# Expert weights loaded by halves of the contraction, and one DVE step moved, in a two-layer mixer and mixture-of-experts kernel

## What is computed

```python
def moe(x, router_w, router_bias, w_gate, w_up, w_down, sw_gate, sw_up, sw_down):
    ...                       # 8 of 64 experts for each token, by sigmoid scores in groups
    def expert_block(args):
        b_tok, b_w, e = args
        xb = xt[b_tok]
        h = jax.nn.silu(xb @ w_gate[e]) * (xb @ w_up[e])        # 1024 -> 256
        return (h @ w_down[e]) * b_w[:, None].astype(xt.dtype)  # 256 -> 1024
    ...
    shared = (jax.nn.silu(xt @ sw_gate) * (xt @ sw_up)) @ sw_down
    return (routed + shared).reshape(bsz, s, d)
```

## Time and profile before

| | |
|---|---|
| median of three runs (lowest to highest) | 1270.3 us (1269.92 to 1272.2) |
| the profiled execution: own time, span | 1272.9 us, 1271.2 us |
| PE busy | 1167.8 us, 92% |
| DVE, ACT busy | 486.9 us, 193.4 us |
| DMA | 463.78 MB, 365 GB/s over the span |
| PE clock granted | 0.996 of full on average |

### The profile page before, as it was taken

The page is one execution under the profiler, slowest core; times in us unless marked ns, Lnnn a source line. Parts: engine busy times, 40 slices in busy tenths (PEclk is TensorE's granted clock), DMA queues, the critical chain, the costliest instruction groups (busy, mean ns, idle before and its releaser), DMA issues.

```text
span 1271.2 us, 17795 instructions
## 1 busy us (share of the span) xinstructions
PE 1167.8 (92%) x7237; PEld 569.4 (45%) x7237; DVE 486.9 (38%) x1053; ACT 193.4 (15%) x330; POOL 46.7 (4%) x76
## 2 busy tenths in 40 slices
PE   9999999988889888888899999999888998888886
PEld 7774743433333333332387657333333333333332
DVE  5894633333323222322237255332223233322224
ACT  3231211111111111110122312111111111111102
POOL 6200100000000000000010001000000000000000
PEclk9999999999999999999999999999999999999999
DMA  9775969999999999999953277999999999999993
GB/s 345 200 297 191 421 264 421 421 420 421 421 420 423 422 421 421 423 419 421 401 177 135 103 291 312 369 420 421 420 422 421 421 422 421 422 422 421 421 421 137
DMA packets 76125, 463.78 MB, mean 365 GB/s; under 512 B 8544, under 2 KB 9888, under 8 KB 25376
## 3 DMA queue, kind: packets, MB, share of 16 engines
q1 hardware_dynamic: 75920, 462.37, 89.5%
q10 hardware_dynamic: 144, 0.52, 0.1%
HBM read 456.51 MB, written 6.36 MB: 364 GB/s over the span
## 4 chain that ended last, share of the span: by engine, by line
DMA 47%; PE 46%; SPq 3%; DVE 2%; issue 1%; ACT 1%; DVEq 0%
DMA expert_weights<-in_exp_w_up 43%; PE bank L1115 21%; PE bank L646 4%; PE bank L1150 3%; PE bank L632 3%; PE bank L720 2%; PE bank L736 2%; SPq L303 2%; DMA weight_ring<-in_sh_w_down 2%; PE bank L993 1%; DMA expert_weights<-s_rows 1%; PE bank L747 1%; PE bank L1081 1%; PE bank L1070 1%; PE bank L1042 1%
## 5 line engine op out<-in xcount | busy, mean ns | idle before, releaser
L1115 PE MATMUL bank<-expert_weights,weight_ring 128*64 128x512 f32 x1536 | 342.8, 594 | 34.3 <-DMA expert_weights<-in_exp_w_up 34.3
L1150 PE MATMUL bank<-expert_weights,hiddenT 128*32 128x512 f32 x2048 | 233.0, 595 | 15.7 <-ACT weight_ring L1362 8.5
L1115 PEld LDWEIGHTS bank<-expert_weights,weight_ring 128*64 128x64 f32 x1536 | 123.9, 137 | 246.2 <-issue 245.9
L1968 DVE TENSOR_TENSOR hidden<-silu_gate,bank 128x256 f32<-128x256 f32 x64 | 27.0, 421 | 439.2 <-ACT silu_gate L1371 439.2
L1115 PE MATMUL bank<-expert_weights,hT 128*64 128x512 f32 x512 | 120.3, 612 | 40.2 <-DMA expert_weights<-in_exp_w_up 40.2
L1150 PEld LDWEIGHTS bank<-expert_weights,hiddenT 128*32 128x32 f32 x2048 | 60.7, 109 | 143.0 <-issue 117.7
L1371 ACT ACTIVATE silu_gate<-bank 128x256 f32<-128x256 f32 x64 | 24.6, 385 | 486.0 <-PE bank L1115 486.0
L1115 PEld LDWEIGHTS bank<-expert_weights,hT 128*64 128x64 f32 x512 | 40.2, 139 | 120.6 <-issue 120.6
L1978 DVE TENSOR_SCALAR y_top<-bank,slot_gate 128x512 fp32r<-128x512 f32 x64 | 48.1, 751 | 97.5 <-PE bank L1150 97.5
L1375 ACT ACTIVATE y_top<-bank,slot_gate 128x512 fp32r<-128x512 f32 x64 | 44.0, 688 | 254.6 <-PE bank L1150 254.6
L1985 DVE SCALAR_TENSOR_TENSOR y_low<-bank,slot_gate,y_top 128x512 fp32r<-128x512 f32 x64 | 48.1, 751 | 57.6 <-ACT y_top L1375 57.6
(11 more groups left out here) (375 smaller groups left out, 982.6 us busy)
## 6 DMA issues: line engine op xcount, KB each, us to landing
expert_weights<-in_exp_w_gate SPq DMA_DIRECT2D x128, 1024.0 KB, 15.0
expert_weights<-in_exp_w_up SPq DMA_DIRECT2D x128, 1024.0 KB, 17.1
expert_weights<-in_exp_w_down SPq DMA_DIRECT2D x128, 1024.0 KB, 19.0
weight_ring<-in_w_in_even SPq DMA_DIRECT2D x5, 2048.0 KB, 10.1
weight_ring<-in_w_out SPq DMA_DIRECT2D x4, 2048.0 KB, 7.9
weight_ring<-in_w_in_odd SPq DMA_DIRECT2D x4, 2048.0 KB, 10.4
s_c<-expert_weights SPq DMA_DIRECT2D x1, 3072.0 KB, 9.8
expert_weights<-s_c SPq DMA_DIRECT2D x1, 3072.0 KB, 10.4
```

Source lines behind the costliest of these rows:

```text
L1115: last_mm = nc.tensor.matmul(bank[6][a * 2 * CAP:(a + 1) * 2 * CAP, :].rearrange("p (w f) -> p w f", w=2), octet_tokens(l, v, c)[:, 2 * q ...
L1150: last_mm = nc.tensor.matmul(bank[b][by_tile:by_tile + CAP, :], hm[:, j, own:own + CAP], ew_d(2 * u + a)[:, j, half * 512:(half + 1) * 512 ...
L1968: nc.vector.tensor_tensor(hslot[:, :], sg[:, :], bank[6][:, DE:2 * DE], ALU.mult)\
```

## The change

Gate and up weights are loaded in halves: `expert_half` issues 512 KB for gate and 512 KB for up, chunks 0 to 3 (part 0) or 4 to 7 (part 1), 4 KB for each partition. Part 0 of both experts of a pair comes first and counts on `gu_in[u]`, part 1 on `gu_rest[u]`; `gu_in`, `gu_rest` and `d_in` are now one semaphore for a pair. TensorE waits for `gu_in` ahead of chunk 0 and for `gu_rest` ahead of chunk 4. The refills are written out: `first_refill` issues part 0 once the first four chunks of the first product are done (`gu_half`), part 1 at `gu_full`; `last_refill` also loads the down weights of the last pair in two column halves (`down_half`, rows of 2 KB), and the last down product waits for its second half at `d_rest`. In `dve_mix0` the second half of `dve_s5_inputs` moves behind the decay scores. Extra passes over the experts (`npass` over 1) are not run with these inputs.

```diff
-        def expert_load(sp, m, l, e, s):
+        def expert_half(sp, l, e, s, part, landed):
+
+            lo, hi = part * EW // 2, (part + 1) * EW // 2
             src_g = A["exp_w_gate"][l, e].rearrange("(p c) f -> p (c f)", c=KC)
             src_u = A["exp_w_up"][l, e].rearrange("(p c) f -> p (c f)", c=KC)
-            sp.dma_start(ew[:, s, 0:EW], src_g).then_inc(m["gu_in"][s], 16)
-            sp.dma_start(ew[:, s, EW:2 * EW], src_u).then_inc(m["gu_in"][s], 16)
+            sp.dma_start(ew[:, s, lo:hi], src_g[:, lo:hi]).then_inc(landed, 16)
+            sp.dma_start(ew[:, s, EW + lo:EW + hi], src_u[:, lo:hi]).then_inc(landed, 16)
+
+        def down_half(sp, l, e, s, part, landed):
+
+            src = A["exp_w_down"][l, e].rearrange("(p j) n -> p j n", j=JE)
+            sp.dma_start(ew_d(s)[:, :, part * 512:(part + 1) * 512], src[:, :, part * 512:(part + 1) * 512])\
+              .then_inc(landed, 16)
...
         def first_load(sp, m, l, s):
-            expert_load(sp, m, l, s, s)
-            sp.dma_start(ew[:, s, 2 * EW:3 * EW], down_src(l, s)).then_inc(m["d_in"][s], 16)
+            expert_half(sp, l, s, s, 0, m["gu_in"][s // 2])
+            expert_half(sp, l, s, s, 1, m["gu_rest"][s // 2])
+            sp.dma_start(ew[:, s, 2 * EW:3 * EW], down_src(l, s)).then_inc(m["d_in"][s // 2], 16)
...
+            def refill(base, it, u):
+
+                sp.wait_ge(m["gu_full"], (base - 1) * 2 + u + 1)
+                for part, landed in ((0, m["gu_in"]), (1, m["gu_rest"])):
                     for s in (2 * u, 2 * u + 1):
-                        expert_load(sp, m, l, it * NSLOT + s, s)
-                    sp.wait_ge(m["y_hi_full"], (base - 1) * 2 + u + 1)
-                    for s in (2 * u, 2 * u + 1):
-                        sp.dma_start(ew[:, s, 2 * EW:3 * EW], down_src(l, it * NSLOT + s)).then_inc(m["d_in"][s], 16)
...
+                        expert_half(sp, l, it * NSLOT + s, s, part, landed[u])
+                sp.wait_ge(m["y_hi_full"], (base - 1) * 2 + u + 1)
+                for s in (2 * u, 2 * u + 1):
+                    sp.dma_start(ew[:, s, 2 * EW:3 * EW], down_src(l, it * NSLOT + s)).then_inc(m["d_in"][u], 16)
+
+            def first_refill(ps):
+
+                sp.wait_ge(m["gu_half"], ps + 1)
+                for s in range(2):
+                    expert_half(sp, l, NSLOT + s, s, 0, m["gu_in"][0])
+                sp.wait_ge(m["gu_full"], ps * PAIRS + 1)
+                for s in range(2):
+                    expert_half(sp, l, NSLOT + s, s, 1, m["gu_rest"][0])
...
+            def last_refill(ps):
+
+                sp.wait_ge(m["gu_full"], ps * PAIRS + PAIRS - 2)
+                for part, landed in ((0, m["gu_in"]), (1, m["gu_rest"])):
+                    for s in (2, 3):
+                        expert_half(sp, l, NE - NSLOT + s, s, part, landed[1])
+                sp.wait_ge(m["y_hi_full"], ps * PAIRS + PAIRS - 2)
+                for s in (2, 3):
+                    down_half(sp, l, NE - NSLOT + s, s, 0, m["d_in"][1])
+                for s in (2, 3):
+                    down_half(sp, l, NE - NSLOT + s, s, 1, m["d_rest"])
...
-                        for a in range(2):
-                            pe.wait_ge(m["gu_in"][2 * u + a], 32 * g + 32)
+                        pe.wait_ge(m["gu_in"][u], 64 * g + 64)
                         for c in range(KC):
                             if opening:
                                 pe.wait_ge(m["xg_hi" if c % 2 else "xg_lo"], n + c // 2 + 1)
+                            if c == KC // 2:
+                                pe.wait_ge(m["gu_rest"][u], 64 * g + 64)
...
+                            if opening and c == KC // 2 - 1:
+                                last_mm.then_inc(m["gu_half"], 1)
...
+                            if ending and q == 3 and half:
+                                pe.wait_ge(m["d_rest"], 32 * ps + 32)
...
-            dve_s5_inputs(dve, chain)
+            dve_s5_inputs(dve, chain, 0)
...
+            dve_s5_inputs(dve, chain, 1)
             dve.wait_ge(*B.read("r1"))
```

More of the change, by code:

```diff
@@ L197, in build @@
         for l in range(2):
[L198 to L199 removed]
+            for name in ("gu_in", "d_in", "gu_rest"):
+                MO[l][name] = [sem(f"moe{l}_{name}{u}") for u in range(2)]
+            MO[l]["d_rest"] = sem(f"moe{l}_d_rest")
+            MO[l]["gu_half"] = sem(f"moe{l}_gu_half")
         ring_in = [sem(f"ring_in{i}") for i in range(2)]
@@ L410, in sp_moe @@
-            with sp.Fori(1, NE // NSLOT) as it:
-                group(it, it)
+                        expert_half(sp, l, it * NSLOT + s, s, part, landed[u])
[9 more added lines that the diff above has]
+                    expert_half(sp, l, NSLOT + s, s, 1, m["gu_rest"][0])
+                sp.wait_ge(m["y_hi_full"], ps * PAIRS + 1)
+                for s in range(2):
+                    sp.dma_start(ew[:, s, 2 * EW:3 * EW], down_src(l, NSLOT + s)).then_inc(m["d_in"][0], 16)
@@ L412, in sp_moe, with refills @@
+            def refills(ps):
+                first_refill(ps)
+                refill(ps * (NE // NSLOT) + 1, 1, 1)
+                with sp.Fori(2, NE // NSLOT - 1) as it:
+                    for u in range(2):
+                        refill(ps * (NE // NSLOT) + it, it, u)
+                refill(ps * (NE // NSLOT) + NE // NSLOT - 1, NE // NSLOT - 1, 0)
+                last_refill(ps)
+            refills(0)
             sp.wait_ge(m["npass"], 1)
@@ L415, in sp_moe @@
                 with sp.Fori(1, npass) as ps:
-                    with sp.Fori(0, NE // NSLOT) as it:
-                        group(ps * (NE // NSLOT) + it, it)
+                    for u in range(2):
+                        refill(ps * (NE // NSLOT), 0, u)
+                    refills(ps)
             return npass
@@ L1677, in dve_s5_powers, with dve_s5_inputs @@
               .then_inc(M1["powers"], 1)
-        def dve_s5_inputs(dve, chain):
+        def dve_s5_inputs(dve, chain, half):
             mul = lambda out, x, y: nc.vector.tensor_tensor(out, x, y, ALU.mult)
@@ L1685, in dve_s5_inputs @@
             br, bi = (R5["raw"][:, w, :].unsqueeze(1).broadcast_to([P, 2, 512]) for w in range(2))
-            for half in range(2):
-                gr, gi = (R5["bt"][:, 2 * half:2 * half + 2, w, :] for w in range(2))
-                mul(R5["tmp"], gi, bi)
-                chain.link(mul(R5["tmp_d"], gi, br))
-                mul(gi, gr, bi)
-                chain.link(mul(gr, gr, br))
-                nc.vector.tensor_tensor(gi, gi, R5["tmp_d"], ALU.add)
-                last = nc.vector.tensor_tensor(gr, gr, R5["tmp"], ALU.subtract)
-                last.then_inc(M1["bt"], 1)
-                dve.wait_ge(M1["bt"], half + 1)
+            gr, gi = (R5["bt"][:, 2 * half:2 * half + 2, w, :] for w in range(2))
+            mul(R5["tmp"], gi, bi)
+            chain.link(mul(R5["tmp_d"], gi, br))
+            mul(gi, gr, bi)
+            chain.link(mul(gr, gr, br))
+            nc.vector.tensor_tensor(gi, gi, R5["tmp_d"], ALU.add)
+            last = nc.vector.tensor_tensor(gr, gr, R5["tmp"], ALU.subtract)
+            last.then_inc(M1["bt"], 1)
+            dve.wait_ge(M1["bt"], half + 1)
         def dve_s5_outputs(dve, chain):
```

8 lines of the change are left out of this document (1 added, 7 removed).

## The result

The changed kernel takes **1288.23 us**, median of 4 runs (1286.37 to 1288.92), beside 1270.42 us of the kernel before on the same chip: ratio 1.0137, 95% interval 1.0123 to 1.0151. It is 17.8 us slower, where 6.7 us less were forecast.

What follows compares the result with a forecast made beforehand. Each MoE was taken as bound by its expert-weight DMA stream at 421 GB/s, TensorE elsewhere. 1.7 + 1.5 + 3.5 - 2.1 + 1.5 + 3.5 = 9.6, less 2.9, is 6.7 us: 1270.3 becomes 1263.6 us, range 1259.5 to 1269.0.

Steps and rivals of the forecast that it cites:

- Shorter rows: Gate and up loads in both expert streams: 4 KB rows run at 419 GB/s in place of 421, 2.9 us lost.
- the number of DMAs: Refills: SyncE issues 8 DMAs for 4, some 4 us, under a pair's 14.9 us; no loss in the sum.
- the far end: Far end of the cost of short DMAs in the streams: 13 ns a row, 4.2%, 25 us, 1285.8 us.
- DVE order: First mixer: a copy put ahead of the second S5 input half removes TensorE's wait before line 646, 1.7 us gained.
- First refill on half a product: Start of each MoE: the first refill, issued after half the first product, starts the stream sooner, 1.5 us gained each.
- The hole in SyncE's queue: Sign to look for: after the early first refill, a hole of about 2 us in the queue near 182.6 to 184.6.
- Halves at the end: End of each MoE: 16 matmuls in place of 32 stand behind the last landing, 3.5 us gained each.
- The second mixer gives back 2.1: Start of the second mixer: line 661 waits for the S5 tables behind the stream, 2.1 us lost.
- So some 4 us in place of 2: SyncE's time to issue a refill's 8 DMAs for 4, under the 14.9 us that a pair lasts.
- Each short DMA costs by itself: Rival, streams: 240 more DMAs, each with its completion; 413 GB/s, loss 11.6 us, 1272.3 us; chance 0.10.
- A fixed time for each row: Rival, streams: at 3.7 ns a row the halved loads cost 1.2%, 7.1 us for 2.9: 1267.8 us; chance 0.08.
- The clock: Rival, second mixer: TensorE's clock falls in the new 2.1 us wait, 1.7 us more, 1265.3 us; chance 0.20.

Runs made afterwards that it cites:

- e16: The kernel before, unchanged, profiled once more: 1269.87 us.
- e6: The changed kernel with gate and up loads cut by even and odd partitions, 512 KB DMAs with 8 KB rows: 1274.17 us, ratio 1.0032.
- e3: The changed kernel with each gate and up refill DMA taking the same half of both experts, 1 MB in 4 KB rows: 1283.84 us, ratio 1.0107.
- e12: The kernel before with one edit, gate and up refills in 1 MB DMAs of 4 KB rows: 1289.89 us, ratio 1.0147.
- e5: The changed kernel with gate and up refills by quarters for both experts, 512 KB DMAs in 2 KB rows: 1320.22 us, ratio 1.0394.
- e1: The kernel before with the new DVE order of the first mixer alone: 1270.41 us beside 1270.44, ratio 0.9998.
- e11: The kernel before with gate and up by halves in the last two refills of a MoE, old DVE order: 1267.98 us, ratio 0.9977.
- e10: The kernel before with the new DVE order and gate and up by halves in the last two refills of a MoE: 1267.61 us, ratio 0.9972.
- e14: The kernel before with the last two refills by halves and the second mixer's S5 tables issued earlier, old DVE order: 1268.16 us, ratio 0.9978.
- e13: The kernel before with new DVE order, last two refills by halves, and the second mixer's S5 tables issued earlier: 1268.05 us, ratio 0.9977.
- e4: The changed kernel with gate and up cut by partitions 0 to 63 and 64 to 127, 512 KB DMAs with 8 KB rows: 2182.68 us, ratio 1.7173.
- e2: The changed kernel with halves only in the first and last refill of a MoE, other loads whole 1 MB: 1268.23 us, ratio 0.9981.
- e8: The kernel before with the new DVE order and only the last refill of gate and up by halves: 1268.49 us, ratio 0.9984.
- e9: The changed kernel with the first four loads of each MoE whole, all refills by halves: 1286.45 us, ratio 1.0123.
- e7: The changed kernel with halves only in first and last refills, and the S5 tables issued behind the last product's first half: 1268.32 us, ratio 0.9979.

## Why the prediction was wrong, step by step

**Shorter rows: 2.9 us forecast, about 18 measured. This is the step that failed.** The mechanism was named, its size was off sixfold, and the number of DMAs, taken as free, cost about 5 us more. Spacing of a pair, each from its second MoE:

| kernel | rows, DMA size | first and last start, steps | us a pair |
|---|---|---|---|
| before (e16) | 8 KB, 1 MB | 1033.15, 1152.53, 8 | 14.92 |
| e6 | 8 KB, 512 KB | 1035.22, 1154.62, 8 | 14.93 |
| e3 | 4 KB, 1 MB | 1041.58, 1147.96, 7 | 15.20 |
| e12 | 4 KB, 1 MB | 1050.61, 1157.08, 7 | 15.21 |
| changed | 4 KB, 512 KB | 1043.97, 1150.40, 7 | 15.20 |
| e5 | 2 KB, 512 KB | 1051.12, 1146.00, 6 | 15.81 |

A pair's gate and up weights are 32 rows of 8 KB on each of 16 engines. Rows of 4 KB add 32 for 0.28 us, 8.8 ns a row; rows of 2 KB add 96 for 0.89 us, 9.3 ns. I took 1.5 ns, from "419 GB/s over 92 to 95". In windows of 1 us the same trace reads:

```profile
91.00:92.00 1.00, 1.00 (x4) 0.48 (x3) 0.51 (x1) 0.98 (x2) 0.00 (x0) 1.00 0.97 401
92.00:93.00 1.00, 1.00 (x3) 0.38 (x2) 0.97 (x2) 0.69 (x1) 0.00 (x0) 1.00 1.04 426
93.00:94.00 1.00, 1.00 (x4) 0.47 (x3) 1.00 (x3) 0.00 (x0) 0.00 (x0) 1.00 1.00 414
94.00:95.00 1.00, 1.00 (x4) 0.48 (x3) 1.00 (x3) 0.00 (x0) 0.00 (x0) 1.00 1.02 418
```

A window of 3 us among such numbers can't tell 0.5% from 2%. The pair of rows that gave 13 ns was nearer, and I had put it at the far end (1285.8 us).

What I overlooked stands in the same trace. Its DMA view counts the rows; queue q1 over 92 to 95, then over 200 to 600, of which 4 and 2571 are under 512 B:

```profile
q1 hardware_dynamic: 311, 1.26, 102.0%
...
q1 hardware_dynamic: 23108, 168.25, 101.1%
```

That is at most 159.5 ns for a row of 4 KB (102.0% of 16 engines' 3 us over 307 rows) and at most 315.1 ns for one of 8 KB, so 4 to 5 ns that don't scale. The trace also holds each row's own time, and there the commonest values are 84 ns at 2 KB, 159 at 4 KB, 309 at 8 KB, 460 at 12 KB and 611 at 16 KB: 9 ns in every row, whatever its length. At 9 ns the 32 rows of 60 pairs would have given 17.3 us.

The Trainium skill ("DMA: Bandwidth & Descriptors", Why small descriptors are slow) has a fixed cost in every packet, and so the right sign. Its 3 cycles made 1.2% of the halved loads; the runs show 0.28 us on 9.96 us, those loads of a pair (4.19 MB at 421 GB/s), 2.8%. By its rules for kernel authors (1 MiB or more per DMA) e3 should beat the changed kernel and e6 lose to the kernel before: they do, by 4.4 and 3.3 us, but not in the spacing.

**The account.** Against e16, whose 1269.87 us is nearer the median than the first profile's 1272.9, the changed kernel's span is 17.8 us longer (1286.0 for 1268.2), which is also what the medians say. By the starts in both traces (the changed kernel's rows stand in the first section, its first products at 161.75 and 798.18, its last down product at 1269.15; these are e16's, with its last down product at 1251.30):

```profile
161.91 1.51 PE L1115 MATMUL bank<-expert_weights,weight_ring 128*64 128x512 f32 x6
...
616.96 3.65 PE L1115 MATMUL bank<-expert_weights,hT 128*64 128x512 f32 x16 [1.83 <-DMA expert_weights<-in_exp_w_up]
...
626.07 3.64 PE L1150 MATMUL bank<-expert_weights,hiddenT 128*32 128x512 f32 x32
635.72 1.20 PE L661 MATMUL bank<-expert_weights,gathered_xT 128*32 128x96 f32 x48
...
787.02 1.51 PE L1115 MATMUL bank<-expert_weights,weight_ring 128*64 128x512 f32 x6
...
1242.17 3.65 PE L1115 MATMUL bank<-expert_weights,hT 128*64 128x512 f32 x16 [1.85 <-DMA expert_weights<-in_exp_w_up]
```

| stretch | before | changed | us |
|---|---|---|---|
| to the first product | 161.91 | 161.75 | -0.2 |
| first MoE to its last landing | 455.05 | 465.68 | +10.6 |
| landing to down product | 9.11 | 5.68 | -3.4 |
| down product to second mixer | 9.65 | 12.31 | +2.7 |
| second mixer to the second MoE | 151.30 | 152.76 | +1.5 |
| second MoE to its last landing | 455.15 | 465.29 | +10.1 |
| landing to down product | 9.13 | 5.68 | -3.5 |

The sum is +17.8. Of 10.6 and 10.1, e12 has 9.0 and 8.9 (163.67 to 627.74 and 799.58 to 1263.63): rows alone. e3 has 7.4 and 7.9, from 161.90 and 796.43 to these last landings:

```profile
624.35 3.65 PE L1164 MATMUL bank<-expert_weights,weight_ring 128*64 128x512 f32 x16 [1.58 <-DMA expert_weights<-in_exp_w_up]
...
1259.43 3.65 PE L1164 MATMUL bank<-expert_weights,weight_ring 128*64 128x512 f32 x16 [1.49 <-DMA expert_weights<-in_exp_w_up]
```

So the halved first refill and the start on half a product give 1.6 and 1.1 back, and doubling the DMAs costs 3.2 and 2.3. It does so once, before the tenth product (changed 255.72 to 286.33 over two pairs, e3 255.94 to 283.73), not in each pair. The windows place half of it at the first two refills, where the queue is empty or nearly so. These are 35 us from the first refill on and the 90 us behind them, in the changed kernel, then in e3:

```profile
165.30:200.30 35.00, 34.35 (x223) 13.77 (x223) 10.70 (x23) 4.29 (x8) 0.00 (x0) 1.00 0.95 347
200.30:290.30 90.00, 85.22 (x534) 31.82 (x526) 30.14 (x60) 10.64 (x19) 0.00 (x0) 1.00 1.02 413
```

```profile
165.45:200.45 35.00, 34.38 (x223) 13.81 (x223) 10.70 (x23) 4.29 (x8) 0.00 (x0) 1.00 0.96 366
200.45:290.45 90.00, 86.73 (x542) 32.67 (x536) 30.14 (x60) 10.63 (x19) 0.00 (x0) 1.00 1.02 413
```

19 GB/s over 35 us are 0.67 MB, 1.6 us of the 3.2; in the second MoE it is 353 against 366 GB/s, 1.1 of the 2.3. Why a DMA of 512 KB moves less there, and where the rest goes, is open.

**What the 24.5 us between forecast and measurement are made of.** The rows 15.0 (17.9 for 2.9). The number of DMAs 5.5, a term that the prediction put at nothing: it had SyncE's issues "under the 14.9 us that a pair lasts" and gave no time to the DMAs at the first refill. The DVE order 1.7, the start of the second MoE 1.5, and 0.8 in the terms that came out nearly right.

**DVE order: 1.7 forecast, 0.0 measured** (e1; e11 against e10, e14 against e13 within 0.4 us). The step itself works: in the changed kernel's profile DVE waits 2.25 us for the same load, and TensorE runs through. But the wait that it removes belongs to executions in which s_rows lands late: 2.1 to 2.6 us of DVE wait in 7 of the 18 profiles of this case (the first, the changed kernel's, e4, e5, e6, e11 and e12), 0.73 us or less in the others. In the late ones TensorE stops for 1.25 to 1.67 us under the old order (before, e11, e12) and not at all under the new, so there the step may be worth its 1.7 (the first expert product starts at 161.75 in the changed kernel, at 163.88 in the first profile of before); the medians don't show it. I had written down that the profiled execution was 2.6 us over the median, and then took a gain from that very excess.

**First refill on half a product: 1.5 forecast for each MoE.** In e3, with 1 MB DMAs, it came, 1.6 and 1.1. With the 512 KB DMAs of the change it did not: in the first MoE of e2 the thirtieth product starts 425.3 us behind the first, in e16 425.2, and in e10, which has no such refill, 425.0. The hole in SyncE's queue is there as described; what the early start gains, the small DMAs seem to lose again behind it.

**Halves at the end: 3.5 for each MoE.** In the changed kernel it holds to 0.1 us (the account). In a stream at the old rate it does not: the last product's wait was 1.83 us, and a product can't gain more than it waits. With one refill by halves TensorE's own chain takes over (e8); with two the second MoE gives 3.3 (from its first product to the start of the last 16 matmuls e10 has 787.70 to 1243.02, e16 787.02 to 1245.63).

**The second mixer gives back 2.1: right, 2.6.** More: with 8 KB rows and halves at the end the second mixer starts between 635.10 (e8) and 636.45 (e11), in e16 at 635.72, so the end of the first MoE is worth 0.6 us at most as long as the tables stand behind the stream.

**Missed altogether: +1.5 at the second MoE.** "So some 4 us in place of 2" for SyncE's issues was wrong: it is held up to 5 us at one issue. The shared down weights, issued 1 us late and behind fuller queues, are waited for 1.8 us, and with the first loads whole they are not (e9).

**The rivals.** "Each short DMA costs by itself" had the right sign and nearly the right rate: under 412.6 GB/s it gave over 1272.8 us, and the halved loads run at 410 (4.19 MB in 9.96 + 0.28 us). But the owner is the row, since e6 has as many DMAs at 421. "A fixed time for each row" had the mechanism, with 3.7 ns as its price and a chance of 0.08. The clock did not fall in the changed kernel's new wait (48 matmuls in 1.20 us after 2.58 us idle), but it did in e10's (2.15 us).

**A better version.** e10, 1267.61 us, is 0.28% under before and 1.6% under the change: whole 1 MB loads of 8 KB rows, and halves in the last two refills alone. e2, e7, e8, e11, e13 and e14 can't be told from it.

## What to carry to other kernels

Where a stage is one saturated stream, an edit to the form of its loads is multiplied by the whole stream: price the fixed time in a row first, over tens of microseconds and from product starts, and cut only the loads whose landing somebody waits for. A wait is worth at most its own length, and only if it is there in the typical execution; when the profiled one lies above the median, profile it twice before believing a wait of 2 us. The number of DMAs cost nothing inside the full stream here (e6), but 1.0 to 3.2 us where a stream starts. A held issue queue is not a slow stream: ask what is queued behind it.

## What the hardware showed that I had not expected

- A DMA that writes 64 neighbouring partitions keeps the engines busy (0.97) at 199 GB/s, under half of 421; on every second partition it runs at 421 (e4, e6). Between 300 and 600 a row of 8 KB took 631 ns on average in e4 and 313 in e6. The Trainium skill ("DMA: Bandwidth & Descriptors", The descriptor swizzle) has partitions 0 to 63 written through half of the 16 ports, which fits; no run here shows a port.
- A row costs 8.8 to 9.3 ns beyond its bytes, the same at 4 and 2 KB, and the trace of before has 9 ns in the rows' own times.
- SyncE's issues are held when much is under way, and by the traces rows count there more than DMAs. Where an issue of over 1.5 us ended inside the streams, the rows issued and not done were 1110 in the changed kernel, 1315 in e3 and 1360 in e5 (medians), in 9, 7 and 6 DMAs; e6 had up to 12 DMAs under way, but with about 1000 rows at most, and was held only at the ends of its streams. It isn't the whole rule: in e4 the median is 515 rows, and in the changed kernel's second refill an issue takes 1.75 us (184.11) with about 5 DMAs under way. No run varied it by itself.
- Products behind a wait of about 2 us run at half clock in some executions and not in others: after 2.03 us 3.65 us and, in e6, 5.35 us (1244.77). Each such product behind the stream's last wait costs 1.7 us, which may be part of the scatter of these kernels (e2 alone ran from 1265.2 to 1271.0 us); no run tests that.
